# Value products of a pair of heads moved one pair later, into the middle of the next gate, in a hybrid attention layer

## Chip, cores, metric

One core of one Trainium2 chip. The metric is the device time of one execution in microseconds. Before the change the median of three runs is 424.05 us (423.93 to 424.34).

## The reference, cut to what matters

One layer on 256 tokens of width 1024, all in float32. One input projection gives queries, keys and values for two attention branches of 8 heads of 64 each, and two sigmoid gates of width 1024:

```
proj = rmsnorm(x, g_mix) @ w_in        # [MoBA q,k,v | stick-breaking q,k,v | gate_moba | gate_sb]
y_a = merge_heads(moba_attention(qa, ka, va)) @ w_br_moba
y_b = merge_heads(stick_breaking_attention(qb, kbh, vbh)) @ w_br_sb
x = x + (sigmoid(ga) * y_a + sigmoid(gb) * y_b) @ w_out
```

With 256 tokens the MoBA branch is one causal block with a softmax and ALiBi. The stick-breaking branch takes softplus of the scores, a cumulative sum over keys, and an exponential, which gives its weights. Each branch then multiplies its weights with its values: these are the value products of the title. A cross-attention into 256 memory tokens and an MLP of width 4096 follow.

## The kernel before, in words

**Precision.** Every large float32 product is three matmuls on a high and a low part. ScalarE (ACT) writes the high part of a weight chunk of 128x2048 numbers (`split` at line 437, helper line 435), VectorE (DVE) the rest (`split` at line 689, helper line 683), and TensorE (PE) multiplies. Chunks arrive by DMA from the SP queue in a ring of six (`raw`, where the low part replaces the chunk), and the high parts have a ring of four (`w_hi`).

**The stage of the change.** Chunks 12 to 19 are the eight gate chunks. A loop over `p` = 0 to 3 handles two gate chunks and one pair of heads of either branch. PE's order in a turn, written out by hand (lines 1244 to 1282):

- `gate(2p)`, 48 matmuls (line 1228), into bank 0;
- the cumulative sums of the stick-breaking scores, 8 matmuls (lines 1258 to 1261), in banks 4 and 5;
- six transposes of the MoBA weights `mo_u` (line 1269), into banks 6 and 3;
- the first half of `gate(2p+1)`, 24 matmuls, into bank 1;
- `scores(p+1)` (lines 1187 to 1204), the scores of the next pair for both branches, in banks 2 to 5;
- the second half of `gate(2p+1)`;
- `attended(p)` (line 1240): the value products, from `mo_pT` (transposed MoBA weights) and `sb_aT` (stick-breaking weights) with `v_tok`, into bank 7, `ATT_O`. It raises the semaphore `sb_av` by one.

After the loop PE goes on with chunk 20 (`MK[0]`, line 1286), and then the branch projections (chunks 21 to 24), which need `att_lo` at 4.

**ACT in a turn** (lines 516 to 525): the exponential that writes `sb_aT` (line 520), which waits for the cumulative sums and, before it overwrites the tile, for `attended(p-1)`; the high part of chunk 16+2p; the softplus and the MoBA exponentials of the next pair (`softplus_exp`, lines 490 to 503); `att_high(p)` (line 482), which reads bank 7 after `attended(p)`; the high part of chunk 17+2p.

**DVE in a turn** (lines 815 to 828): `gate_out(2p)` (line 811), the copy of the transposes into `mo_pT` (line 821), the low part of chunk 16+2p, the scores work of the next pair (lines 777 to 796), `gate_out(2p+1)`, `att_low(p)` (line 767, helper line 683), the low part of chunk 17+2p.

Each engine takes its instructions in the order written; the semaphores tie the orders together. No DMA stands in this loop outside the SP queue, which has the loads alone; GpSimd has nothing here.

Of the kernel before, what the change touches and what calls it, by code (L numbers as in the profile page):

```python
# [21 lines left out]
P = 128  # L22
# [35 lines left out]
def hybrid_layer(nc, x, head0, head, chunk1, chunk2, mem, memT, g_final, weights, ff, out):  # L58
    fp32, f32r = mybir.dt.float32, mybir.dt.float32r
    ACT, ALU = mybir.ActivationFunctionType, mybir.AluOpType  # L60
# [5 lines left out]
    HEADS, DH = 8, 64  # L66
# [52 lines left out]
    with ctx:  # L119
# [13 lines left out]
        def sb(name, shape, dt=fp32, over=None):  # L133
            return place(name, shape, dt, over)[0]
# [14 lines left out]
        raw, o = place("raw", [P, RAW, CH])  # L149
# [30 lines left out]
        xs = sb("xs", [P, TOK, D], over=o)  # L180
        memT_raw = sb("memT_raw", [P, KT, SEQ], over=o)
        mem_tok = sb("mem_tok", [P, TOK, D], over=o + 8192)

        o = at[0]
        aT_hi_all, _ = by_tokens("aT_hi", 0, 192)
# [62 lines left out]

        banks = ctx.enter_context(nc.psum_tensor("bank", [P, 8, 512], fp32))
        bank = [banks[:, i, :] for i in range(8)]  # L250
        MO_S, MO_PT, SB_Z, ATT_O = (2, 3), (6, 3), (4, 5), 7
        WARM_UP = 8
        V_BANKS, MV_BANKS, X_S, X_PT = ((0, 1), (6, 7)), (5, 2), (0, 1, 3, 6), (7, 4, 3, 6)
        X_ROW_BANK, MEM_ROW_BANK = 7, 1
# [166 lines left out]
        def flat(t):  # L421
            return t.rearrange("p b t -> p (b t)")


        @block.scalar
        def _(act):
# [10 lines left out]
            def split(c):  # L437
                split_hi(c % RING, c % RAW, 16 * (c // RAW + 1), c - RING + 1 if c >= RING else None)
# [40 lines left out]
            def att_high(p):  # L479

                act.wait_ge(sb_av, p + 1)
                copy(aT_hi[:, p:p + 5:4, :], bank[ATT_O].rearrange("p (b q) -> p b q", b=2), ACT.Copy)\
                    .then_inc(att_hi, 1)
# [31 lines left out]
            split(15)  # L515
            for p in range(HEADS // 2):
                act.wait_ge(sb_c, p + 1)
                if p:
                    act.wait_ge(sb_av, p)
                copy(sb_aT[:, :, :], banks[:, SB_Z[0]:SB_Z[1] + 1, 0:384], ACT.Exp).then_inc(sb_exp, 1)  # L520
                split(GATE0 + 2 * p + 4)
                if p + 1 < HEADS // 2:
                    softplus_exp(p + 1)
                att_high(p)
                split(GATE0 + 2 * p + 5)

            act.wait_ge(gate_evac, 8)
            for n in range(2):
# [141 lines left out]
        def _(dve):  # L670
# [18 lines left out]
            def split(c):  # L689
                split_lo(c % RING, c % RAW, c + 1)  # L690
# [74 lines left out]
            def att_low(p):  # L765
                dve.wait_ge(att_hi, p + 1)
                low(aT_lo[:, p:p + 5:4, :], bank[ATT_O].rearrange("p (b q) -> p b q", b=2), aT_hi[:, p:p + 5:4, :])\
                    .then_inc(att_lo, 1)
# [40 lines left out]
            def gate_out(h):  # L809
                dve.wait_ge(w_used, GATE0 + h + 1)  # L810
                nc.vector.tensor_tensor(gateT[:, 2 * h:2 * h + 2, :], halves_of(bank[h % 2][:, :]),
                                        twice(rstd_row[:, :]), ALU.mult).then_inc(gate_evac, 1)

            dve.wait_ge(lo_done[MEM], KT)
            for p in range(HEADS // 2):
                gate_out(2 * p)
                dve.wait_ge(mo_t, p + 1)
                if p:
                    dve.wait_ge(sb_av, p)
                for i in range(2):  # L820
                    last = nc.vector.tensor_copy(mo_pT[:, i, :], bank[MO_PT[i]][:, 0:384])
                last.then_inc(mo_pt, 1)
                split(GATE0 + 2 * p + 4)
                if p + 1 < HEADS // 2:
                    scores(p + 1)
                gate_out(2 * p + 1)
                att_low(p)
                split(GATE0 + 2 * p + 5)
            split(24)

            def mem_k_out(i, b):
# [259 lines left out]
        def _(pe):  # L1091
# [87 lines left out]
            def scores(p):  # L1179

                if p:
                    pe.wait_ge(mo_pt, p)
                    pe.wait_ge(sb_exp, p)
                heads = [(i, slice(DH * i, DH * i + DH)) for i in range(2)]
                for i, r in heads:
                    q, k = qkT[r, p, :], qkT[r, 4 + p, :]
                    mm(bank[MO_S[i]][:, 0:128], q[:, 0:P], k[:, 0:P], start=True, stop=True)
                for i, r in heads:
                    q, k = qkT[r, p, :], qkT[r, 4 + p, :]
                    last = mm(bank[MO_S[i]][:, 128:384], q[:, P:SEQ], k, start=True, stop=True)  # L1190
                last.then_inc(mo_s, 1)
                for i, r in heads:
                    q, k = qkT[r, 8 + p, :], qkT[r, 12 + p, :]
                    mm(bank[SB_Z[i]][:, 0:256], k[:, 0:P], q, start=True, stop=False, skip_group_check=True)
                for i, r in heads:
                    q, k = qkT[r, 8 + p, :], qkT[r, 12 + p, :]
                    mm(bank[SB_Z[i]][:, 256:384], k[:, P:SEQ], q[:, P:SEQ], start=False, stop=False,
                       skip_group_check=True)


                if p == 0:
                    pe.wait_ge(masks_ready, 2)
                for i in range(2):
                    last = mm(bank[SB_Z[i]][:, 0:384].rearrange("p (b q) -> p b q", b=3)[:, 0:3:2, :], ident_r[:, :],
                              future_r[:, :, :], start=False, stop=False, skip_group_check=True)
                last.then_inc(sb_z, 1)
# [15 lines left out]
            def gate(h, m):  # L1222
                c = GATE0 + h
                for kk in range(KT):
                    a = kk * 256 + m * P
                    wh, wl = w_hi[:, c % RING, a:a + P], w_lo[:, c % RAW, a:a + P]
                    for n, (w, v) in enumerate(((wh, hT_hi), (wh, hT_lo), (wl, hT_hi))):
                        last = mm(halves(h % 2)[m], w, v[:, kk, :], start=kk == 0 and n == 0,  # L1228
                                  stop=kk == KT - 1 and n == 2)
                return last  # L1230

            def attended(p):
                o = bank[ATT_O]
                for b, a_ in enumerate((mo_pT, sb_aT)):
                    if b == 1:
                        pe.wait_ge(sb_exp, p + 1)
                    for kt, (qa, qb, ka, kb) in enumerate(((0, 256, 0, 256), (128, 256, 256, 384))):
                        for i in range(2):
                            v0 = b * WIDTH + DH * (2 * p + i)
                            last = mm(o[DH * i:DH * i + DH, SEQ * b + qa:SEQ * b + qb], v_tok[:, kt, v0:v0 + DH],  # L1240
                                      a_[:, i, ka:kb], start=b == 0 and kt == 0, stop=kt == 1, skip_group_check=True)
                last.then_inc(sb_av, 1)

            for p in range(HEADS // 2):
                if p == 0:
                    pe.wait_ge(v_evac, 2)
                    spread_rstd(MEM_ROW_BANK, 2)
                else:
                    pe.wait_ge(gate_evac, 2 * p - 1)
                pe.wait_ge(w_lo_ready, GATE0 + 2 * p + 1)  # L1250
                gate(2 * p, 0)
                gate(2 * p, 1).then_inc(w_used, 1)

                pe.wait_ge(sp_lo_done, p + 1)
                for i in range(2):
                    z = bank[SB_Z[i]]
                    for sp in (sp_hi, sp_lo):
                        mm(z[:, 128:256], neg_ones_r[:, :], sp[:, i, 256:384], start=False, stop=False,
                           skip_group_check=True)
                    mm(z[:, 0:384], neg_tri_r[:, :], sp_hi[:, i, :], start=False, stop=False, skip_group_check=True)  # L1260
                    last = mm(z[:, 0:384], neg_tri_r[:, :], sp_lo[:, i, :], start=False, stop=True,
                              skip_group_check=True)
                last.then_inc(sb_c, 1)
                pe.wait_ge(mo_normed, p + 1)
                if p == 0:
                    pe.wait_ge(v_evac, 4)
                for i in range(2):
                    for j in range(3):
                        t = tr(bank[MO_PT[i]][:, P * j:P * j + P], mo_u[:, i, P * j:P * j + P], ident[:, :])  # L1269
                t.then_inc(mo_t, 1)  # L1270

                pe.wait_ge(*((gate_evac, 2 * p) if p else (row_ready, 2)))
                pe.wait_ge(w_lo_ready, GATE0 + 2 * p + 2)
                gate(2 * p + 1, 0)
                if p + 1 < HEADS // 2:
                    scores(p + 1)
                gate(2 * p + 1, 1).then_inc(w_used, 1)

                pe.wait_ge(mo_pt, p + 1)
                if p:  # L1280
                    pe.wait_ge(att_lo, p)
                attended(p)


            pe.wait_ge(lo_done[MEM], KT)
# [161 lines left out]
```

## Time and profile before

| what | us |
|---|---|
| median of 3 runs | 424.05 |
| lowest, highest | 423.93, 424.34 |
| the profiled execution's own time | 423.02 |
| its span, first to last instruction | 420.9 |
| PE busy | 409.4 (97% of the span) |
| DVE busy | 335.8 (80%) |
| ACT busy | 250.8 (60%) |

The span is what the trace covers; the profiled execution's own time has 2.1 us more around it. Busy shares are means over stages with different limits, so the argument has to be made from the stage of the change, which lies from about 76 to 141 us of the span.

### The profile page before, as it was taken

What the parts mean: (1) busy time and instruction counts of PE and PEld (TensorE: products, weight loads), DVE (VectorE), ACT (ScalarE), POOL (GpSimd) and SP (SyncE); (2) the same over time, 40 slices, a digit from 0 to 9 for tenths busy, and PEclk for the clock granted to TensorE, in tenths of its full rate; (3) what the DMA queues carried; (4) which work ended last, traced back from release to release, by engine and by line L of the source; (5) the groups of instructions that cost most, each with busy time, mean ns of one, the idle gap of its engine ahead of it and who ended that gap; (6) DMA issues with size and microseconds to landing.
All of it is one profiled execution on the core that took longest, in us unless ns stands there. A gap on an engine that the chain in (4) does not pass through costs nothing.

```text
span 420.9 us, 7064 instructions
## 1 busy us (share of the span) xinstructions
PE 409.4 (97%) x2839; PEld 376.5 (89%) x2839; DVE 335.8 (80%) x446; ACT 250.8 (60%) x300; POOL 27.5 (7%) x39
## 2 busy tenths in 40 slices
PE   8999999999999999999999999999999999999992
PEld 8999978999999999889988898899999999999971
DVE  6587566967757437875856899999999999999976
ACT  7664228773665634652556368877777777776723
POOL 0079200000000000000200000000000000000002
PEclk9999999999999999999999999999999999999998
DMA  8999545433234255555352345466555555554002
GB/s 297 421 416 379 199 188 182 154 145 123 101 112 188 101 201 200 201 186 179 135 202 100 106 176 178 153 213 208 204 202 208 202 207 205 201 206 183 2 0 100
DMA packets 12539, 77.47 MB, mean 184 GB/s; under 512 B 1376, under 2 KB 1376, under 8 KB 4064
## 3 DMA queue, kind: packets, MB, share of 16 engines
q1 hardware_dynamic: 12512, 77.09, 50.7%
q8 instruction: 19, 0.31, 0.3%
q14 instruction: 8, 0.07, 0.0%
HBM read 76.04 MB, written 1.05 MB: 183 GB/s over the span
## 4 chain that ended last, share of the span: by engine, by line
PE 88%; DVE 6%; ACT 2%; issue 2%; DMA 1%; POOL 0%; POOLq 0%; DVEq 0%; ACTq 0%
PE bank L1114 39%; PE bank L1133 16%; PE bank L1380 15%; PE bank L1228 11%; PE bank L1240 1%; DVE res L1045 1%; PE bank L1326 1%; DVE t_lo L683 1%; PE bank L1346 1%; DVE t_sum L940 1%; DVE f_lo L683 1%; PE bank L1147 1%; DMA head_all<-in_head_dram 1%; PE bank L1269 1%; DVE w_lo L683 1%
## 5 line engine op out<-in xcount | busy, mean ns | idle before, releaser
L683 DVE TENSOR_TENSOR w_lo<-raw,w_hi 128x2048 fp32r<-128x2048 f32 (+2 forms) x87 | 147.9, 1708 | 26.4 <-ACT w_hi L435 25.4
L1114 PE MATMUL bank<-hT_hi,w_hi 128*128 128x256 f32 x416 | 117.2, 282 | 0.7 <-DVE hT_lo L695 0.4
L1114 PE MATMUL bank<-hT_hi,w_lo 128*128 128x256 f32 x416 | 116.7, 281 | 0.0
L1114 PE MATMUL bank<-hT_lo,w_hi 128*128 128x256 f32 x416 | 116.3, 280 | 0.0
L1114 PEld LDWEIGHTS bank<-hT_hi,w_hi 128*128 128x128 f32 x416 | 78.3, 188 | 1.9 <-issue 0.6
L435 ACT ACTIVATE w_hi<-raw 128x2048 fp32r<-128x2048 f32 x33 | 62.8, 1914 | 27.3 <-PE bank L1114 13.8
L1114 PEld LDWEIGHTS bank<-hT_lo,w_hi 128*128 128x128 f32 x416 | 78.3, 188 | 0.6
L1114 PEld LDWEIGHTS bank<-hT_hi,w_lo 128*128 128x128 f32 x416 | 78.2, 188 | 0.0
L1228 PE MATMUL bank<-hT_hi,w_hi 128*128 128x256 f32 x128 | 36.8, 288 | 0.0
L683 DVE TENSOR_TENSOR t_lo<-t_sum,t_hi 128x1024 fp32r<-128x1024 f32 x30 | 36.5, 1218 | 0.0
L1228 PE MATMUL bank<-hT_hi,w_lo 128*128 128x256 f32 x128 | 36.0, 282 | 0.0
L1228 PE MATMUL bank<-hT_lo,w_hi 128*128 128x256 f32 x128 | 35.7, 279 | 0.0
L615 ACT ACTIVATE f_hi<-forms 128x896 fp32r<-128x896 f32 (+1 forms) x16 | 15.2, 947 | 26.1 <-DVE forms L986 25.6
L581 ACT ACTIVATE w_hi<-raw 128x2048 fp32r<-128x2048 f32 x16 | 30.3, 1903 | 0.0
L588 ACT ACTIVATE w_hi<-raw 128x1536 fp32r<-128x1536 f32 (+1 forms) x16 | 24.0, 1501 | 1.4 <-PE bank L1133 1.4
L1228 PEld LDWEIGHTS bank<-hT_hi,w_hi 128*128 128x128 f32 x128 | 24.1, 188 | 0.5 <-issue 0.5
L1228 PEld LDWEIGHTS bank<-hT_lo,w_hi 128*128 128x128 f32 x128 | 24.2, 189 | 0.0
L1228 PEld LDWEIGHTS bank<-hT_hi,w_lo 128*128 128x128 f32 x128 | 24.0, 188 | 0.0
L1380 PE MATMUL bank<-t_hi,f_hi 128*128 128x512 f32 x60 | 23.4, 390 | 0.0
L1380 PE MATMUL bank<-t_hi,f_lo 128*128 128x512 f32 x60 | 23.4, 389 | 0.0
L1380 PE MATMUL bank<-t_lo,f_hi 128*128 128x512 f32 x60 | 23.3, 389 | 0.0
L600 ACT ACTIVATE t_hi<-t_sum 128x1024 fp32r<-128x1024 f32 x15 | 15.9, 1062 | 9.9 <-DVE t_sum L947 9.9
(195 smaller groups left out, 823.4 us busy)
## 6 DMA issues: line engine op xcount, KB each, us to landing
raw<-in_weights_dram SPq DMA_DIRECT2D x65, 1024.0 KB, 4.8
head_all<-in_head_dram SPq DMA_DIRECT2D x7, 256.0 KB, 4.0
raw<-in_chunk_dram SPq DMA_DIRECT2D x4, 256.0 KB, 5.0
raw<-in_chunk_dram SPq DMA_DIRECT2D x2, 512.0 KB, 6.5
res<-in_x_dram SPq DMA_DIRECT2D x2, 512.0 KB, 11.3
mem_tok<-in_mem_dram SPq DMA_DIRECT2D x1, 1024.0 KB, 12.1
memT_raw<-in_memT_dram SPq DMA_DIRECT2D x1, 1024.0 KB, 10.9
out_dram<-xs SPq DMA_DIRECT2D x2, 512.0 KB, 2.7
```

The lines of the kernel that those rows point to most:

```text
L435: copy(w_hi[:, slot, :], raw[:, rslot, :], ACT.Copy).then_inc(w_hi_ready, 1)
L581: copy(w_hi[:, c % RING, :], raw[:, c % RAW, :], ACT.Copy).then_inc(up_hi, 1)
L588: copy(w_hi[:, c % RING, 0:cols], raw[:, c % RAW, 0:cols], ACT.Copy).then_inc(down_hi, 1)
L600: copy(t_hi[:, u % 2, 2 * H:4 * H], t_sum[:, u % 2, 2 * H:4 * H], ACT.Copy).then_inc(t24_hi, 1)
L615: copy(f_hi[:, u % 2, first:upto * P], forms[:, first:upto * P], ACT.Copy).then_inc(f_hi_done, 1)
L683: return nc.vector.tensor_tensor(dst, whole, high.bitcast(fp32), sub)
L940: nc.vector.tensor_tensor(blocks(t_sum[:, u % 2, 0:2 * H], H), blocks(b[:, 0:2 * H], H), b12, ALU.add)\
L1045: return nc.vector.scalar_tensor_tensor(s, src, scale[:, t:t + 1], s, ALU.mult, ALU.add)
L1114: last = mm(outs[m], w, v[:, k0 + k, :], start=first and n == 0, stop=k == nk - 1 and n == 2, skip_group_check=bool(kt_wait))
L1133: last = mm(outs[t][c], s, w[:, k * cols + 512 * c:k * cols + 512 * c + 512], start=start and k == 0 and n == 0, stop=stop and k == nk - 1 ...
L1228: last = mm(halves(h % 2)[m], w, v[:, kk, :], start=kk == 0 and n == 0, stop=kk == KT - 1 and n == 2)
L1380: last = mm(bank[p], s, w[:, n * H:n * H + H], start=start and j == 0, stop=u == PAIRS - 2 and p in (P1, P6, P7) and j == 2, skip_group_ch ...
```

## The change

`attended(p-1)` moves from the end of turn p-1 to the middle of turn p, behind the transposes of pair p and ahead of `scores(p+1)`; the last one, of pair 3, stays behind the loop. The transposes move behind the first half of `gate(2p+1)`, and their second bank is now 0 in place of 3. On ACT `att_high` and on DVE `att_low` follow one turn later, and DVE makes the low part of chunk 16+2p ahead of the copy into `mo_pT`. Pair 1 gets a tile of its own for its stick-breaking weights (`sb_aT1`, in the upper part of `gateT`); pairs 0, 2 and 3 share `sb_aT`.

```diff
+        sb_aT1 = sb("sb_aT1", [P, 2, 384], over=o + 12288)
...
-        MO_S, MO_PT, SB_Z, ATT_O = (2, 3), (6, 3), (4, 5), 7
+        MO_S, MO_PT, SB_Z, ATT_O = (2, 3), (6, 0), (4, 5), 7
...
+        def sb_weights(p):
+            return sb_aT1 if p == 1 else sb_aT
...
             for p in range(HEADS // 2):
                 act.wait_ge(sb_c, p + 1)
+                if p == 1:
+                    act.wait_ge(sumsq_dve, 2)
+                if p >= 2:
+                    act.wait_ge(sb_av, 2 * p - 3)
+                copy(sb_weights(p)[:, :, :], banks[:, SB_Z[0]:SB_Z[1] + 1, 0:384], ACT.Exp).then_inc(sb_exp, 1)
+                split(GATE0 + 2 * p + 4)
                 if p:
-                    act.wait_ge(sb_av, p)
-                copy(sb_aT[:, :, :], banks[:, SB_Z[0]:SB_Z[1] + 1, 0:384], ACT.Exp).then_inc(sb_exp, 1)
-                split(GATE0 + 2 * p + 4)
+                    att_high(p - 1)
                 if p + 1 < HEADS // 2:
                     softplus_exp(p + 1)
-                att_high(p)
                 split(GATE0 + 2 * p + 5)
+            att_high(HEADS // 2 - 1)
...
             for p in range(HEADS // 2):
+                if p == HEADS // 2 - 1:
+                    dve.wait_ge(sb_av, 2)
                 gate_out(2 * p)
+                split(GATE0 + 2 * p + 4)
+                if p:
+                    att_low(p - 1)
                 dve.wait_ge(mo_t, p + 1)
                 if p:
                     dve.wait_ge(sb_av, p)
                 for i in range(2):
                     last = nc.vector.tensor_copy(mo_pT[:, i, :], bank[MO_PT[i]][:, 0:384])
                 last.then_inc(mo_pt, 1)
-                split(GATE0 + 2 * p + 4)
                 if p + 1 < HEADS // 2:
                     scores(p + 1)
                 gate_out(2 * p + 1)
-                att_low(p)
                 split(GATE0 + 2 * p + 5)
+            att_low(HEADS // 2 - 1)
...
             def scores(p):
                 if p:
-                    pe.wait_ge(mo_pt, p)
+                    pe.wait_ge(mo_normed, p)
                     pe.wait_ge(sb_exp, p)
...
+            def attend(p):
+                pe.wait_ge(mo_pt, p + 1)
+                if p:
+                    pe.wait_ge(att_lo, p)
+                attended(p)
+
             for p in range(HEADS // 2):
+                if p:
+                    pe.wait_ge(mo_pt, p)
...
                 last.then_inc(sb_c, 1)
+                pe.wait_ge(*((gate_evac, 2 * p) if p else (row_ready, 2)))
+                pe.wait_ge(w_lo_ready, GATE0 + 2 * p + 2)
+                gate(2 * p + 1, 0)
                 pe.wait_ge(mo_normed, p + 1)
+                pe.wait_ge(gate_evac, 2 * p + 1)
...
                 t.then_inc(mo_t, 1)
-
-                pe.wait_ge(*((gate_evac, 2 * p) if p else (row_ready, 2)))
-                pe.wait_ge(w_lo_ready, GATE0 + 2 * p + 2)
-                gate(2 * p + 1, 0)
+                if p:
+                    attend(p - 1)
                 if p + 1 < HEADS // 2:
                     scores(p + 1)
                 gate(2 * p + 1, 1).then_inc(w_used, 1)
 
-                pe.wait_ge(mo_pt, p + 1)
-                if p:
-                    pe.wait_ge(att_lo, p)
-                attended(p)
+            attend(HEADS // 2 - 1)
```

## Rows read from the trace of the kernel before

**Rows 1.** The page: the span, and the busy time of each engine.

```profile
span 420.9 us, 7064 instructions
PE 409.4 (97%) x2839; PEld 376.5 (89%) x2839; DVE 335.8 (80%) x446; ACT 250.8 (60%) x300; POOL 27.5 (7%) x39
```

**Rows 2.** Waits of PE over the whole span: us in total, times, longest.

```profile
PE bank L1155 <- DVE zeros L733: 1.1, 1, 1.1
```

**Rows 3.** The chain that ended last, 107 to 141 us: start, us, what.

```profile
107.82 1.45 PE bank L1240 x16
...
119.76 0.42 PE bank L1187 x4
...
121.70 2.83 PE bank L1228 x24
124.53 1.45 PE bank L1240 x16
125.98 5.85 PE bank L1228 x48
...
132.98 0.65 PE bank L1269 x6
133.63 5.66 PE bank L1228 x48
139.29 1.45 PE bank L1240 x16
140.74 28.46 PE bank L1114 x240
```

**Rows 4.** Timeline of PE at 91 us: start, us, what.

```profile
90.84 0.28 PE L1228 MATMUL bank<-hT_hi,w_lo 128*128 128x256 f32 x1
91.05 0.87 PE L1240 MATMUL bank<-mo_pT,v_tok 128*64 128x256 f32 x8
```

**Rows 5.** Timeline of ACT, turns 2 and 3 and behind the loop.

```profile
133.02 0.81 ACT L520 ACTIVATE sb_aT<-bank 128x768 f32<-128x768 f32 x1 [3.93 <-PE bank L1261]
133.72 1.91 ACT L435 ACTIVATE w_hi<-raw 128x2048 fp32r<-128x2048 f32 x1
140.79 0.60 ACT L482 ACTIVATE aT_hi<-bank 128x512 fp32r<-128x512 f32 x1 [5.15 <-PE bank L1240]
```

**Rows 6.** Timeline of DVE, turns 2 and 3 and behind the loop.

```profile
118.96 2.29 DVE L683 TENSOR_TENSOR w_lo<-raw,w_hi 128x2048 fp32r<-128x2048 f32 x1 [0.97 <-ACT w_hi L435]
121.16 0.28 DVE L777 CUSTOM_DVE_ANT_0 mo_u<-bank,alibi 128x128 f32<-128x128 f32 x1
...
124.34 0.96 DVE L785 SCALAR_TENSOR_TENSOR sb_sp<-bank,sb_t 128x768 f32<-128x768 f32 x1 [1.78 <-ACT sb_t L494]
...
127.23 0.95 DVE L683 TENSOR_TENSOR sp_lo<-sb_sp,sp_hi 128x768 fp32r<-128x768 f32 x1
...
128.70 0.68 DVE L683 TENSOR_TENSOR aT_lo<-bank,aT_hi 128x512 fp32r<-128x512 f32 x1
129.30 2.28 DVE L683 TENSOR_TENSOR w_lo<-raw,w_hi 128x2048 fp32r<-128x2048 f32 x1
131.87 0.69 DVE L811 TENSOR_TENSOR gateT<-bank,rstd_row 128x512 f32<-128x512 f32 x1 [0.29 <-PE bank L1228]
133.67 1.02 DVE L821 COPY mo_pT<-bank 128x384 f32<-128x384 f32 x2 [1.11 <-PE bank L1269]
135.67 2.29 DVE L683 TENSOR_TENSOR w_lo<-raw,w_hi 128x2048 fp32r<-128x2048 f32 x1 [0.97 <-ACT w_hi L435]
```

**Rows 7.** Stretches behind PE's last matmul: busy of each engine, PEclk, DMA.

```profile
413.20:418.20 5.00, 0.00 (x0) 0.00 (x0) 3.82 (x7) 2.50 (x7) 2.41 (x3) 1.00 0.26 105
418.50:420.90 2.40, 0.00 (x0) 0.00 (x0) 0.00 (x0) 0.00 (x0) 0.00 (x0) 0.50 0.54 218
```

**Rows 8.** Timeline of PE at the start of the span.

```profile
1.11 3.78 PE L1155 MATMUL bank<-zeros 128*128 128x128 f32 x16 [1.11 <-DVE zeros L733]
5.19 0.44 PE L1114 MATMUL bank<-hT_hi,w_hi 128*128 128x256 f32 x1 [0.29 <-DVE w_lo L683]
```

More of the change, by code:

```diff
@@ L1233, in attended @@
                 o = bank[ATT_O]
-                for b, a_ in enumerate((mo_pT, sb_aT)):
+                for b, a_ in enumerate((mo_pT, sb_weights(p))):
                     if b == 1:
```

## The prediction, made before the changed kernel ran

> **What bounds the kernel now.** I read the page first: PE is busy 409.4 of 420.9 us, and no other engine comes near [rows 1]. A share can hide waits, so the waits of PE come next: the longest of the whole span is 1.1 us, at its start [rows 2], and none lies in the stage of the change. Then the chain of work that ended last. From 76 to 169 us it is made of PE alone, piece behind piece [rows 3]: one turn of the loop, from one start of the value products to the next, is 124.53 - 107.82 = 16.71 us. What the reader is to see there is that each piece starts where the one before it ended. So in this stage only PE's own work and what PE waits for count, and a new wait of PE counts in full. ACT and DVE wait for PE: ACT sat idle 3.93 us before the exponential of pair 3 [rows 5]. Such idle time is what could cover work that comes later.
>
> **What the change removes: changes of form on PE.** The value products use half of the array's columns (64), the gates all 128. The chain shows the price: the 48 matmuls of gate 6, right behind value products, take 5.85 us, the 48 of gate 7, behind transposes, 5.66 [rows 3]. So leaving the 64-column form costs 0.19 us. Entering it has a small price too: between gate matmuls the step is 2.83 / 24 = 0.118 us, from the last gate matmul to the first value product 0.21 us [rows 3, 4], 0.09 more. After the change three of four groups of value products (pairs 0, 1, 2) stand between the transposes and the scores. They are still entered from a 128-column form, and what follows them (the scores, 64 rows by 128 columns) is entered from another form in both kernels. The exit at 0.19 falls away three times: 3 x 0.19 = 0.57 us. What the step from 64 columns to 64 rows costs no row shows. At best scores follow value products as if they were one group, and the entry of 0.09 goes too: 0.84 us saved. At worst it costs as much as the exit: nothing saved. I take 0.57, as the entry into the scores is paid now too. The number of matmuls is the same, and moving the transposes, full width among full width, costs nothing: gate 7 behind them has 5.66 like two halves of 2.83.
>
> **Turns 1 and 2: the new waits are covered.** Let A be the end of the value products in the middle of a turn. Only then can ACT read bank 7 (0.57 to 0.60 us, 0.05 behind A) and DVE make the low part (0.60 to its next start), and behind that in DVE's order stands the copy into `mo_pT`, 1.02 [rows 5, 6]: A + 2.3. PE needs that copy when it starts the next gate, behind the scores (121.70 - 119.76 = 1.94) and half a gate (2.83) [rows 3], A + 4.8: 2.5 us to spare. The scores work of the next pair is queued behind the copy on DVE. Before, it ended 128.18 - 121.70 = 6.5 us behind the scores on PE [rows 3, 6]; the cumulative sums now want it half a gate and a gate later, 2.83 + 5.66 = 8.5 us. That the exit and value products no longer lie between takes 1.6 us of cover, and 2 us are left. DVE's scores work now starts 2.3 us behind the start of the scores on PE, before the change 1.4 (121.16 - 119.76); these 0.9 us are absorbed where DVE sat idle 1.78 us for ACT at line 785 [rows 3, 6]. `gate_out(2p)`, now wanted before the transposes because of bank 0, takes 0.69 [rows 6] at the end of a gate, and PE has cumulative sums and half a gate (over 3.9 us) before it asks. Turn 0 has no value products at all, so the same covers hold with more room. DMAs: none is moved; the loads on SP wait for gate chunks used and follow PE.
>
> **Turn 3: a wait with no cover.** Pairs 0, 2 and 3 share one tile of stick-breaking weights. ACT's exponential of pair 3 overwrites the weights of pair 2, so it waits for `sb_av` at 2p - 3 = 3: three groups of value products done. Before the change the third group lay at 124.53, long before that exponential (133.02) [rows 3, 5]. Now it lies in the middle of gate 7. Behind the waiting exponential stand, on ACT, the high part of chunk 22; behind this, on DVE, the low part of chunk 22, then `att_low(2)`, then the copy of pair 3 into `mo_pT`; and for this copy PE waits before its last value products. From the end A of the third group:
> - to the start of the exponential 0.05 (140.79 behind 140.74), and 0.70 to the split behind it (133.72 - 133.02) [rows 3, 5];
> - high part of chunk 22: 1.91, and 0.04 to DVE (135.67 behind 135.63) [rows 5, 6];
> - low part of chunk 22: 2.20 to the next start (121.16 - 118.96) [rows 6];
> - `att_low(2)`: 0.60 (129.30 - 128.70); its high part on ACT is made meanwhile [rows 6];
> - copy: 1.02 [rows 6], and some 0.06 to PE.
>
> Sum 6.58 us. In the meantime PE has only the second half of gate 7, 2.83 us [rows 3] (no scores follow in the last turn). The difference is 3.75 us. The entry of 0.09 into the last value products, which the old chain paid too, runs off inside it: **3.66 us lost**. Five handovers at 0.02 to 0.12 each are uncertain: 3.4 to 4.0. Before the change the last copy was there at 133.67 + 1.02 = 134.69, over 4 us before PE asked at 139.29; that cover is gone.
>
> Does the loss stay? Behind 140.74 PE has 28.46 us in one piece of the chain, and no wait over 1.1 us anywhere [rows 2, 3], so there is no idle time into which it could sink. Behind the last value products `att_high(3)` and `att_low(3)` are covered by chunk 20 on PE (5.66 us), and chunk 22, ready some 5 us behind A, is wanted only behind chunks 20 and 21.
>
> **Sum.** 3.66 - 0.57 = +3.1 us. The profiled execution of before has a span of 420.9 and 423.02 of its own time; with the change 424.0 and 426.1. It lies 1.03 below the median of the runs; against that median, 424.05 + 3.1 = 427.15 us. With the bounds 3.4 - 0.84 = 2.6 and 4.0 - 0 = 4.0: 426.6 to 428.1; with 0.3 us of scatter between runs, 426.3 to 428.4. A measurement of this kernel can tell about 0.2% (0.85 us) from no change.
>
> **Clock, row against rule.** PE stands still 3.7 us. After its last matmul the granted clock was at its full level, 1.00, through five idle microseconds and was at half, 0.50, from 418.5 on [rows 7]. By this row a shorter stop leaves the clock at full, and that is what the sum takes. The Trainium skill (TensorE: Matmul & The Clock Gate, "HAM oscillation") speaks against it: a wait between two bursts of matmuls can let the clock fall back to half, so that the next burst starts slow. By that rule the sum would be 2.0 us more, worked out as a rival below.
>
> **Rivals.**
> 1. *The clock falls in the stop.* PE resumes at 1.2 GHz. At the start of the span, before full clock, the matmuls took 3.78 / 16 = 0.236 us each against 0.65 / 6 = 0.108 of the transposes, also 128 columns; by 5.2 us that was over [rows 3, 8]. If the same 4.1 us of slow work follow, half is lost, 2.0 us: 427.15 + 2.0 = 429.2. For it: the stop is by far the longest inside the span. Against: the row above.
> 2. *The wait is hidden, and only the saved exits count.* This ends not slower. It would need the copy of pair 3 to land before gate 7 ends, so the chain behind A must be at most 2.8 us in place of 6.6; the point from which it decides is whether the exponential of pair 3 really has to wait for the third group. If its wait were met early, it would start at about 133 as now, and DVE's copy, behind chunk 22's low part, would land at about A + 2.3, in time. Then 424.05 - 0.57 = 423.5, or 423.2 at the bound. Against it stands the value 3 and the shared tile; nothing in the profile speaks for it.
> 3. *A second wait in turns 1 and 2.* DVE now blocks on `att_low` before the copy and the scores work. If the scores work came 2 us later than I have it, PE would wait at the cumulative sums of pairs 2 and 3. At one more microsecond each: 429.2. Against: the 2 us of cover above, and 0.9 of idle time left on DVE at line 785.
>
> **Chances.** Forecast 0.80, clock 0.10, hidden 0.06, second wait 0.04. The forecast's own range leaves a little over 2 in 10 out, so the range reaches up to the clock case: 426.3 to 429.3. Hidden is split evenly between the last two outcomes on its side: faster by over 0.2% 0.03, within 0.2% 0.03, slower 0.94.
>
> **What the profile after would show.** Right: in the waits of PE one new row of about 3.7 us, line 1240's group behind the DVE copy into `mo_pT`; in ACT's timeline the last exponential behind PE's value products instead of line 1261's group, some 3 us later in the turn; on DVE one long idle time before the low part of chunk 22; gates 2, 4 and 6 at 5.66 in place of 5.85, a turn near 16.5 us. Wrong: no such wait (then rival 2); a turn that is 16.7 or longer (the 64-to-64 step costs what was saved, or rival 3, told apart by a wait at line 1258); a granted clock of 0.5 behind the stop (rival 1); or a stop that is there while the end moves less, which would mean that a later stage has slack that I did not see.

## The result, and the profile after

The changed kernel takes 429.16 us (median of 4 runs, 429.06 to 430.71), the kernel before 423.99 in the same session: a ratio of 1.0133, 95% interval 1.0114 to 1.0152, slower. The forecast was slower by 3.1 us. By the medians it is slower by 5.2, and by the ratio 5.6, which is more than the top of the stated range (429.3, 5.25 us above 424.05). So the sign and the stop were right, and the size was not. Where the other 2 us came from is the subject of what follows.

The profiled execution of the changed kernel is its slowest run, 430.71 us. First its page (span; busy time of PE and DVE), against [rows 1]:

```profile
span 428.6 us, 7068 instructions
PE 413.1 (96%) x2839; PEld 379.2 (88%) x2839; DVE 335.4 (78%) x446; ACT 251.1 (59%) x300; POOL 25.6 (6%) x39
```

PE has the same 2839 matmuls and is busy 3.7 us longer with them. A stop alone can't do that: something also makes the matmuls slower. About 1 us of it lies at the start of the span, ahead of all that was changed (first line of the table below); the rest is in the stage of the change. The waits of PE, over the whole span (total, times, longest; four rows left out), against [rows 2]:

```profile
PE bank L1252 <- DVE mo_pT L834: 3.6, 1, 3.6
PE bank L1167 <- DVE zeros L741: 1.1, 1, 1.1
...
PE bank L1240 <- DVE mem_row L733: 0.4, 1, 0.4
```

Two rows are new. The first is the stop in turn 3. The last, 0.4 us in turn 0, was not forecast. The others, of 1.1 us and less, stood there before. Now the chain that ended last, turns 2 and 3 (start, us, what), against [rows 3]; line 1252 is the value products, 1240 the gates, 1293 the transposes:

```profile
119.53 1.45 PE bank L1252 x16
120.98 0.42 PE bank L1199 x4
...
122.92 8.48 PE bank L1240 x72
...
132.55 2.83 PE bank L1240 x24
135.38 0.66 PE bank L1293 x6
136.04 1.48 PE bank L1252 x16
...
137.59 0.04 ACT sb_aT L526
137.64 0.67 issue
138.30 1.92 ACT w_hi L439
...
142.45 0.68 DVE aT_lo L691
143.13 0.94 DVE mo_pT L834 x2
...
144.12 2.83 PE bank L1252 x16
```

The chain leaves PE at the end of pair 2's value products, goes through ACT's exponential and its split, through DVE's split, `att_low` and copy, and comes back to PE at 144.12: link by link the queue that the prediction had. And the last 16 value products take 2.83 us in place of 1.45. That is the second loss. The granted clock (windows; columns: busy of PE, PEld, DVE, ACT, POOL, then PEclk, DMA share, GB/s):

```profile
140.60:143.30 2.70, 0.00 (x0) 0.00 (x0) 2.70 (x3) 1.92 (x2) 0.00 (x0) 1.00 0.54 173
143.40:150.20 6.80, 6.08 (x31) 4.99 (x32) 4.15 (x5) 3.17 (x4) 0.00 (x0) 0.50 0.19 81
150.30:153.00 2.70, 2.70 (x25) 2.70 (x25) 0.00 (x0) 0.61 (x1) 0.00 (x0) 1.00 0.00 0
421.30:423.20 1.90, 0.00 (x0) 0.00 (x0) 1.90 (x4) 1.29 (x4) 1.06 (x2) 1.00 0.00 0
```

PE went idle at about 140.5; from 143.4 on the clock is at half (1.2 GHz), through the rest of the stop and 6.1 us of work behind it. Half of 6.1 would be 3.0 us lost in this execution; the table below makes it 2.8. Behind the last matmul the clock stood at full for 5 us in [rows 7]. In this execution, where the last matmul ended at 420.9, the last of these rows has it at full to 423.2, and it was at half from 423.3 on: 2.4 us. In the ten profiles of this document that time is anything from 2.4 to 5.3 us.

ACT's and DVE's timelines of turn 3, against [rows 5, 6]:

```profile
137.59 0.81 ACT L526 ACTIVATE sb_aT<-bank 128x768 f32<-128x768 f32 x1 [7.77 <-PE bank L1252]
138.30 1.91 ACT L439 ACTIVATE w_hi<-raw 128x2048 fp32r<-128x2048 f32 x1
```

```profile
140.24 2.29 DVE L691 TENSOR_TENSOR w_lo<-raw,w_hi 128x2048 fp32r<-128x2048 f32 x1 [7.43 <-ACT w_hi L439]
142.45 0.68 DVE L691 TENSOR_TENSOR aT_lo<-bank,aT_hi 128x512 fp32r<-128x512 f32 x1
143.05 1.01 DVE L834 COPY mo_pT<-bank 128x384 f32<-128x384 f32 x2
```

The exponential waits 7.77 us for PE's value products, where it waited 3.93 for the cumulative sums, and DVE sits idle 7.43 us for the split. Both engines stand still for over seven microseconds. What they then do takes 6.5 us (137.59 to 144.08), and PE has 2.8 us of work meanwhile.

**Where the time went**, in us from matmul start to matmul start. "Scores 0" is the start of the first scores, and so on; chunk 20 follows the last value products, chunk 21 is the first branch projection.

| stretch | before | changed | changed, second profile | own tile | own tile, early mem_row |
|---|---|---|---|---|---|
| first large matmul to scores 0 | 57.30 | 58.34 | 58.26 | 57.98 | 58.18 |
| scores 0 to 1 | 23.79 | 24.41 | 24.41 | 24.41 | 23.78 |
| scores 1 to 2 | 16.71 | 16.50 | 16.50 | 16.50 | 16.50 |
| scores 2 to 3 | 16.71 | 16.51 | 16.51 | 16.51 | 16.51 |
| scores 3 to chunk 20 | 20.98 | 25.97 | 25.45 | 20.98 | 20.98 |
| chunk 20 to 21 | 5.76 | 7.24 | 6.54 | 5.76 | 5.76 |
| chunk 21 to the last matmul | 266.4 | 266.4 | 266.4 | 266.4 | 266.4 |

The first line is no part of the change. Over the ten profiles it lies between 57.30 and 59.16 with the same work there; the kernel before with `mem_row` early, below, has 58.18. Two things move it: the moment at which the full clock begins (5.4 us in the profile of before, 6.9 in that of the changed kernel, 10.4 in the one with 59.16), and waits of up to 0.84 us for the low part of a chunk between 7 and 10 us, which some of the profiles have. So whole times of single profiled executions differ by more than some of the terms here, and the stretches are what to compare. The last line shows that nothing of the loss is given back later. In between stand all the terms: +0.62, -0.21, -0.20, +4.99 and +1.48 in the first profile.

### The profile page after: what moved, and what is told of

Read it like the earlier page. It is cut to its first block, busy times and chain, and to the rows that moved or that the text cites. A ratio compares the mean times of both kernels' runs of the same rounds, so it can differ in the third digit from the quotient of the medians.

```text
span 428.6 us, 7068 instructions
## 1 busy us (share of the span) xinstructions
PE 413.1 (96%) x2839; PEld 379.2 (88%) x2839; DVE 335.4 (78%) x446; ACT 251.1 (59%) x300; POOL 25.6 (6%) x39
## 4 chain that ended last, share of the span: by engine, by line
PE 83%; DVE 7%; ACT 6%; issue 3%; DMA 1%; POOL 0%; POOLq 0%; DVEq 0%; ACTq 0%
PE bank L1126 39%; PE bank L1399 15%; PE bank L1145 13%; PE bank L1240 9%; PE bank L1252 2%; ACT w_hi L439 2%; DVE w_lo L691 1%; DVE res L1057 1%; PE bank L1345 1%; DVE t_lo L691 1%; PE bank L1365 1%; DVE t_sum L952 1%; ACT mT_hi L451 1%; DVE f_lo L691 1%; PE bank L1159 1%
```

## The experiments

Theory at this point: the stop comes from the shared tile and the queue behind the exponential; the time beyond it is the clock, and 0.6 us the new wait in turn 0. Rivals: DVE's new order makes the stop by itself; the excess is contention or a later stage; the half clock was an exception of the one profile. The edits are against the changed kernel, if not said otherwise.

**Own tile for pair 3**, over the queries and keys, which are not read after scores 3:

```diff
+        sb_aT3 = sb("sb_aT3", [P, 2, 384], over=o)
...
-            return sb_aT1 if p == 1 else sb_aT
+            return {1: sb_aT1, 3: sb_aT3}.get(p, sb_aT)
...
-                if p >= 2:
-                    act.wait_ge(sb_av, 2 * p - 3)
+                if p == 2:
+                    act.wait_ge(sb_av, 1)
```

> The changed kernel, but pair 3 has a tile of its own for its stick-breaking weights, over the room of the queries and keys, and its exponential waits for no value products (pair 2's waits for sb_av at 1 as before). Theory (the stop comes from the shared tile, and all that queues behind the waiting exponential): the 3.6 us wait of PE for the DVE copy into mo_pT is gone, the clock stays at full, and what is left is three exits saved (-0.57) and the new wait for mem_row in turn 0 (0.4 to 0.6): 423.7 to 424.2 us, within 0.1% of the kernel before. Rival (DVE's new order, low part of chunk 22 and att_low(2) ahead of the copy, makes the stop by itself): PE still waits some 2 us or more for mo_pT, time over 426 us. Rival (part of the loss comes from elsewhere, as contention or a later stage): over 425 us without any new wait of PE in this stage.

Measured: 424.02 us against 423.95, ratio 1.0004 (0.9995 to 1.0013). The wait for `mo_pT` is gone and the whole loss with it, and in the profile the clock stays at full. DVE's new order alone makes no stop, and there was no loss elsewhere. But no gain is left either. One reason is the wait in turn 0, which is still there (24.41 in the table). The chain in turn 3 shows another (line 1241 is the gates, 1253 the value products here):

```profile
135.76 1.45 PE bank L1253 x16
137.21 3.03 PE bank L1241 x24
140.24 1.45 PE bank L1253 x16
```

The half gate behind pair 2's value products takes 3.03 us, not 2.83. In turn 3 there are no scores, so a gate follows the value products as before, and the exit at 0.2 is paid. Only turns 1 and 2 save one.

**Own tile, and `mem_row` early** (the edit on top of the last one):

```diff
-            split(15)
             spread(mem_row, MEM_ROW_BANK, 2)
+            split(15)
```

> As the kernel with the own tile for pair 3, and DVE makes mem_row before the low part of chunk 15 instead of behind it. Theory (gate 1's first half now asks for mem_row 0.66 us earlier, as the transposes no longer stand before it): the 0.4 us wait in turn 0 is gone too, 0.4 to 0.6 us less than with the own tile alone, 423.2 to 423.6 us, 0.1 to 0.2% faster than the kernel before. Rival (that wait hides in what follows and costs nothing): same time as with the own tile alone.

Measured: 423.51 us, ratio 0.9992 (0.9983 to 1.0001). The stretch from scores 0 to 1 is 23.78 again, 0.63 less: all of it comes back. This is what it had been made of, in the changed kernel's timelines of PE and DVE in turn 0:

```profile
83.53 0.33 PE L1281 MATMUL bank<-sp_lo,neg_tri_r 128*128 128x384 f32 x1
84.22 0.39 PE L1240 MATMUL bank<-hT_hi,w_hi 128*128 128x256 f32 x1 [0.35 <-DVE mem_row L733]
84.44 0.28 PE L1240 MATMUL bank<-hT_lo,w_hi 128*128 128x256 f32 x1
```

```profile
83.74 0.42 DVE L733 COPY mem_row<-bank 128x256 f32<-128x256 f32 x1
```

The gate starts 0.69 us behind the start of the last cumulative sum, where with the early `mem_row` it is 0.17, and its next matmul follows after 0.23 in place of 0.12. That is 0.35 of idle time and 0.27 more for running empty and starting again. By the stretches, what is left over against the kernel before is 0.41 us, the two exits; the ratio's interval just includes no change.

**`mem_row` early in the kernel before**, as a control:

> The kernel before, with mem_row made ahead of the low part of chunk 15 and nothing else. Theory (before the change the transposes hid mem_row, so its early making brings nothing there): 423.95 us, within 0.05% of the kernel before. Rival (the early mem_row is a gain of its own, which the kernel with own tile and early mem_row owes nothing to the change): 0.1% faster.

Measured: 424.10 against 424.24, ratio 0.9999 (0.9989 to 1.0008); scores 0 to 1 at 23.77. There it brings nothing. The wait in turn 0 is a product of the change: the transposes used to hide `mem_row`, and the change moved them behind the half gate that asks for it. In the kernel before, `mem_row` was ready at 83.17, and this half gate began at 83.52 (a line of DVE's timeline, and one of the chain):

```profile
82.75 0.42 DVE L725 COPY mem_row<-bank 128x256 f32<-128x256 f32 x1
```

```profile
83.52 2.83 PE bank L1228 x24
```

**The stop filled with work**: 24 matmuls that nobody reads, ahead of the last value products.

```diff
+            for _ in range(24):
+                mm(bank[2][:, 0:256].rearrange("p (b q) -> p b q", b=2), ident_r[:, :], future_r[:, :, :],
+                   start=True, stop=True)
             attend(HEADS // 2 - 1)
```

> The changed kernel, with 24 extra full-width matmuls of 256 columns into the unused bank 2 between gate 7 and the last value products, so that PE works through 2.8 us of its 3.6 us stop. They compute nothing that is used. Theory (what is lost beyond the stop is the half clock behind it): granted clock stays 1.00 through the stage, the value products of pair 3 still start at the same place behind the DVE copy, time 3.1 us above the kernel before and its saved exits, 427.0 to 427.8 us, 1.5 to 2 us less than the changed kernel although it has more work. Rival (the clock plays no part, the rest is lost to later stages): 429.0 us or more.

Measured: 428.22 us (427.88 to 429.05), ratio 1.0097 (1.0082 to 1.0113). In the profiled execution the full clock was granted from 10.4 us on to the end of the work, and the mean clock of all four runs is 0.995 to 0.997 (windows of this kernel, around the stop):

```profile
144.00:148.00 4.00, 3.25 (x31) 2.59 (x31) 4.00 (x6) 1.19 (x2) 0.00 (x0) 1.00 0.47 195
148.00:151.00 3.00, 3.00 (x28) 3.00 (x27) 0.56 (x1) 2.70 (x3) 0.00 (x0) 1.00 0.00 0
```

More work, and about 1 us less time than without it. From scores 3 to chunk 20 it takes 24.66 us, 3.68 more than before: this is the stop by itself, and the prediction's 3.66. Chunk 20 is at 5.77 again. The time came out 0.4 above the expected range. That range was built on 3.66 - 0.57, so it still counted three exits, and the 0.62 us of turn 0 not; by the table's terms the sum is 423.95 + 0.62 - 0.41 + 3.68 = 427.84, which lies within the interval of the ratio.

**10 matmuls in the stop instead of 24:**

> The changed kernel with 10 extra matmuls in the stop in place of 24, so that 2.4 us of standing still are left of 3.6. Theory (it takes a long stop to bring the clock down): granted clock full in most runs, time as with 24, 427.6 to 428.4 us. Rival (any stop of a few microseconds does it): time as of the changed kernel, 429 us or more, with a mean clock near 0.99.

Measured: 428.91 us (428.21 to 429.33). The wait is 2.4 us. Neither side is right alone: two runs lie at 429.3 with a mean clock of 0.992, two at 428.2 and 428.5 with 0.996. In the profiled one, a slow one, the windows read:

```profile
141.50:144.00 2.50, 0.08 (x2) 0.09 (x4) 2.50 (x5) 0.82 (x1) 0.00 (x0) 1.00 0.73 298
144.30:147.60 3.30, 3.30 (x21) 2.41 (x18) 2.83 (x3) 1.08 (x2) 0.00 (x0) 0.50 0.11 40
```

PE stood still from 141.5 to 143.9, and the clock fell at 144.25, when PE was already at work again. So after a stop of 2.4 us the clock fell in this execution; the mean clocks say that it did so in two runs of four. The two runs are 0.9 us above the other two; by the stretches of the profile the half clock cost 1.6 us in this one (25.68 - 24.66 from scores 3 to chunk 20, 6.32 - 5.77 from there to chunk 21).

**The changed kernel again:**

> The changed kernel once more, beside the others of this call. Theory (stop of 3.6, two exits saved at 0.2, 0.6 for mem_row, and a stretch of half clock behind the stop whose length differs from run to run): 428.7 to 430.7 us, its slowest and fastest run over 1 us apart, mean granted clock below that of the kernel with the stop filled (0.996) by 0.003 or more in all runs. Rival (the half clock of the profiled run was an exception): most runs at clock 0.995 to 0.997 and 427.8 to 428.2 us.

Measured: 429.43 us (429.05 to 429.69), ratio 1.0126 (1.0111 to 1.0142), mean clock 0.992 or 0.993 in all four runs, where the kernel before lies from 0.993 to 0.997. The mean alone does not prove it of a single run, as the ranges touch: the half clock at the start and end of every execution is in it too. But all eight runs of the changed kernel have 0.993 or less and 429.05 us or more, and both profiled ones show the half clock. It is no exception. Its length is not always the same:

```profile
140.50:144.00 3.50, 0.00 (x0) 0.00 (x0) 3.50 (x5) 1.99 (x2) 0.00 (x0) 1.00 0.63 225
144.70:148.00 3.30, 3.30 (x22) 2.60 (x19) 2.83 (x2) 1.54 (x2) 0.00 (x0) 0.50 0.00 0
```

Here it comes 0.6 us behind the end of the stop and lasts 3.4 us, half as long as in the first profile. In the table that is 25.45 - 24.66 = 0.79 and 6.54 - 5.77 = 0.77 us, together 1.6, against 1.31 + 1.47 = 2.8 in the first profile. The expectation of more than 1 us between the slowest and the fastest of these four runs missed (0.6); with the first four, the eight runs lie from 429.05 to 430.71.

**Other order in turn 3, shared tile kept:**

```diff
+                if p == 3:
+                    att_high(p - 1)
                 copy(sb_weights(p)[:, :, :], banks[:, SB_Z[0]:SB_Z[1] + 1, 0:384], ACT.Exp).then_inc(sb_exp, 1)
                 split(GATE0 + 2 * p + 4)
-                if p:
+                if p in (1, 2):
                     att_high(p - 1)
...
                 gate_out(2 * p)
-                split(GATE0 + 2 * p + 4)
+                if p < 3:
+                    split(GATE0 + 2 * p + 4)
...
                 last.then_inc(mo_pt, 1)
+                if p == 3:
+                    split(GATE0 + 2 * p + 4)
```

> The changed kernel with the shared tile kept, but in turn 3 the order is other: on ACT att_high(2) ahead of the exponential, on DVE att_low(2) and the copy into mo_pT ahead of the low part of chunk 22. Theory (not the wait itself but the splits of chunk 22 queued behind it make the stop): from the end of pair 2's value products the copy is done after 0.6 + 0.7 + 1.0 = 2.3 us, the exponential after 0.6 + 0.8 = 1.4, both within the 2.8 us of the half gate: no stop, 423.7 to 424.2 us as with the own tile. Rival (DVE or ACT fall behind for good, and the branch projections wait for chunk 22's or 23's low part): a new wait of PE at line 1126 of up to 2 us.

Measured: 424.25 us against 423.95, ratio 1.0007 (0.9997 to 1.0016), 0.05 above the expected range, and no wait of PE in turn 3. ACT and DVE in its timeline:

```profile
137.94 0.60 ACT L486 ACTIVATE aT_hi<-bank 128x512 fp32r<-128x512 f32 x1 [7.79 <-PE bank L1257]
138.43 0.81 ACT L528 ACTIVATE sb_aT<-bank 128x768 f32<-128x768 f32 x1
139.12 3.73 ACT L439 ACTIVATE w_hi<-raw 128x2048 fp32r<-128x2048 f32 x2
```

```profile
138.56 0.69 DVE L693 TENSOR_TENSOR aT_lo<-bank,aT_hi 128x512 fp32r<-128x512 f32 x1 [5.44 <-ACT aT_hi L486]
139.17 1.01 DVE L837 COPY mo_pT<-bank 128x384 f32<-128x384 f32 x2
141.07 2.29 DVE L693 TENSOR_TENSOR w_lo<-raw,w_hi 128x2048 fp32r<-128x2048 f32 x1 [0.88 <-ACT w_hi L439]
```

ACT waits for the value products as in the changed kernel (7.79 us), and the exponential starts even later behind them, 0.6 us, but the copy is done at 140.2, and the low part of chunk 22 comes behind it. So the wait was not what cost: it was the 4 us of splits queued behind it and ahead of the copy.

**Both last pairs side by side.** On top of own tile and early `mem_row`, the value products of pair 2 stand right before those of pair 3, in bank 2, and pair 3 has a `mo_pT` tile of its own:

```diff
+        mo_pT3 = sb("mo_pT3", [P, 2, 384], over=o + 3072)
...
+        def att_bank(p):
+            return bank[2 if p == 2 else ATT_O]
...
-                if p:
+                if p in (1, 2):
                     attend(p - 1)
...
+            attend(HEADS // 2 - 2)
             attend(HEADS // 2 - 1)
```

(The edit is cut short: `att_high(2)` and `att_low(2)` move behind the loop in the same way, and the waits follow.)

> The kernel with the own tile for pair 3 and the early mem_row, and in turn 3 the value products of pair 2 stand right before those of pair 3, behind gate 7, in bank 2, with a tile of its own for pair 3's transposed MoBA weights. Theory (turn 3 has no scores, so there the moved value products save no exit; side by side they save one exit and one entry): the stretch from the third scores to chunk 20 is 20.7 us in place of 21.0, time 0.3 us less than with the own tile and the early mem_row, 423.2 us, 0.1 to 0.2% below the kernel before. Rival (att_high and att_low of both pairs now come behind each other and the branch projections wait): a wait of PE at line 1126 or so of over 0.3 us and no gain.

Measured: 423.24 us against 424.24, ratio 0.9978 (0.9969 to 0.9988): a little faster than the kernel before, clear of the noise, and far faster than the changed one. The chain of turn 3 (line 1250 the gates, 1262 the value products):

```profile
135.16 0.66 PE bank L1303 x6
135.82 2.82 PE bank L1250 x24
138.64 2.75 PE bank L1262 x32
```

32 value products in one piece take 2.75 us where twice 16 took 2.90, and the half gate is at 2.82. The stretch from scores 3 to chunk 20 is 20.63 in place of 20.98. With the two exits of turns 1 and 2 the terms make 0.21 + 0.20 + 0.35 = 0.76 us; the ratio says 0.9, within its interval.

## Why the prediction was right and wrong

- **PE bounds this stage, a new wait counts in full: right.** 266.4 us behind chunk 21 in every profile.
- **The stop in turn 3: right in place, cause and size.** 3.66 forecast, 3.6 in the waits, 24.66 - 20.98 = 3.68 with the clock held up. Shown by taking away the shared tile, and by putting the splits behind the copy: either removes it.
- **"By this row a shorter stop leaves the clock at full, and that is what the sum takes": this step failed**, and it is the largest miss. One row of five idle microseconds at full clock was read as a bound, and it was none: the clock fell 2.9 us into the stop in one profile, and 0.6 us behind its end in another, both times well under five microseconds of standing still; with 2.4 us of standing still it fell in two runs of four by their mean clocks. Even behind the last matmul, in the place that the row was read from, the changed kernel's profile has 2.4 us in place of 5. With the clock held up by matmuls that nobody reads the kernel takes 428.22 us, which the forecast's range holds, so this step is what took the time out of it. Rival 1 had the right mechanism and, at 2.0 us, about the right price (2.8 and 1.6 in the two profiles, about 1 by the medians with and without filling), with a chance of 0.10, where the two profiles show it and the mean clocks speak for it in all eight runs. The rule of the Trainium skill (TensorE: Matmul & The Clock Gate, "HAM oscillation") that a wait between bursts of matmuls can send the clock back to half, named beside it in the prediction, agrees with these traces (0.50 from 143.4 and from 144.7 us on), and the reading of the row does not.
- **"The exit at 0.19 falls away three times": mis-sized.** The exit measures 0.20 to 0.21, but it falls away twice. The prediction itself noted that "no scores follow in the last turn", and did not draw the conclusion that a gate then follows the value products. 0.41 us saved in place of 0.57. The step from 64 columns to 64 rows costs what was taken: turns of 16.50 and 16.51 against 16.71.
- **"Turn 0 has no value products at all, so the same covers hold with more room": wrong.** Every moved instruction had been cover for something. The 0.66 us of transposes stood between the cumulative sums and gate 1's first half, which asks for `mem_row`; without them PE waits 0.35 us and loses 0.62, a term that the prediction put at nothing. The prediction checked the new waits in turns 1 and 2 and not the old wait (`row_ready` at 2) that the move brought forward.
- **Turns 1 and 2 covered: right.** No wait there, rival 3 did not happen.
- **Sum.** 0.62 - 0.41 + 3.68 = 3.9 us without the clock. With it, 5.5 by the stretches of the second profile and 6.7 by those of the first, which is the slowest of the eight runs; 5.2 by the medians. Forecast was 3.1.

Left open: what decides in one execution whether and for how long the clock falls. It differs between runs of one kernel. A profile shows the fall in two of the eight runs of the changed kernel and in one of the four with 10 matmuls; in the others it is read from the mean clock and not shown directly.

## What to carry to other kernels

When a wait is added, count what stands behind the waiting instruction in its queue and whom that feeds; here two weight splits made a harmless wait into a stop, and a tile over dead memory or another order removed it. When an instruction moves, look also at what it used to cover where it stood. And a stop of TensorE like those here (2.4 and 3.6 us) has to be priced with the clock: its own length, plus the 1.6 to 2.8 us that the half clock cost in the three profiles that show it. One row in which the clock held is no bound.

## What was not expected of the hardware

- A stop of 2.4 us inside a full-clock stretch was followed by half clock in two runs of four, one of 3.6 us in eight of eight (counted by the mean clock; one profile and two show it). In the first profile of the changed kernel PE then did 6.1 us of work at half clock, in the second 3.4. In two of the three profiles the clock fell only when PE was at work again.
- Useless matmuls in the stop made the kernel about 1 us faster (429.16 and 429.43 without, 428.22 with 24; ratios to the kernel before 1.0133 and 1.0126, and 1.0097).
- The PE wait of 0.35 us in turn 0 cost 0.62 on a stream of matmuls.
- The change from 64 columns to the full array costs the following gate 0.20 us (3.03 against 2.83 for half a gate). The scores, 64 rows, cost no more behind value products, 64 columns, than behind a gate: turns 1 and 2 are shorter by 0.21 and 0.20, all of the exit.
